# Joining two query tiles in one batch of scores, in the three attentions with 64-wide heads of a two-block transformer

## The reference

```python
# window: 8 query heads of width 64, 2 key heads; a key counts when |q - k| <= WINDOW (128); a sink joins the sum
s = jnp.einsum('bnqhgd,bnkhd->bnhgqk', qb, kb).astype(jnp.float32) * (ATT_HEAD_DIM ** -0.5)
s = jnp.where(valid[None, :, None, None], s, -jnp.inf)
m = jnp.maximum(jnp.max(s, axis=-1, keepdims=True), sk)
p = jnp.exp(s - m)
p = p / (jnp.sum(p, axis=-1, keepdims=True) + jnp.exp(sk - m))
# memory: 4 heads of width 256, 256 keys
# mla: 8 heads; two products make one score; key chunks up to the query's own
logits = (jnp.einsum('bqhd,bkhd->bhqk', qn, k_nope) + jnp.einsum('bqhr,bkr->bhqk', qp, k_pe))
# dsa: 8 heads of width 64; the 128 best keys of an index score, with a bias for each distance
logits = jnp.einsum('bqhd,bqkhd->bhqk', qb, k_sel).astype(jnp.float32) * scale
```

## Time and profile before

| | |
|---|---|
| Median of 3 runs | 1470.87 us (1466.79 to 1470.9) |
| The profiled execution | 1468.45 us, span 1466.6 us |
| PE busy | 1448.0 us (99%) |
| DVE / ACT / POOL busy | 935.8 / 447.4 / 833.2 us |
| window attention | about 276 to 360 us of the span |
| memory attention | about 496 to 592 us |
| mla attention | about 1123 to 1230 us |
| dsa attention | about 1254 to 1346 us |

### The profile page before, as it was taken

The page is one execution under the profiler, slowest core; times in us unless marked ns, Lnnn a source line. Parts: engine busy times, 40 slices in busy tenths (PEclk is TensorE's granted clock), DMA queues, the critical chain, the costliest instruction groups (busy, mean ns, idle before and its releaser), DMA issues.

```text
span 1466.6 us, 20029 instructions
## 1 busy us (share of the span) xinstructions
PE 1448.0 (99%) x7028; PEld 1149.8 (78%) x7028; DVE 935.8 (64%) x1685; ACT 447.4 (31%) x875; POOL 833.2 (57%) x675
## 2 busy tenths in 40 slices
PE   8999999999999999999999999999999999999998
PEld 7887877766888898788888888887767777667887
DVE  5768887777248334577777763325777786685245
ACT  4556432376122111220010101112333344464112
POOL 4634332534666786467777677776655254444662
PEclk9999999999999999999999999999999999999999
DMA  5211101211333433233333333334224532323332
GB/s 197 88 58 44 58 29 58 72 58 58 115 101 90 122 113 107 63 96 95 93 100 101 97 90 102 113 101 137 87 87 138 93 100 61 112 73 115 101 99 74
DMA packets 37017, 135.60 MB, mean 92 GB/s; under 512 B 4296, under 2 KB 4552, under 8 KB 36296
## 3 DMA queue, kind: packets, MB, share of 16 engines
q1 hardware_dynamic: 33264, 121.13, 27.4%
q10 hardware_dynamic: 3672, 13.35, 3.5%
HBM read 127.64 MB, written 6.82 MB: 92 GB/s over the span
## 4 chain that ended last, share of the span: by engine, by line
PE 89%; DVE 6%; issue 2%; ACT 1%; PEld 1%; DMA 0%; PEldq 0%; DVEq 0%
PE pair L624 25%; PE pair L626 24%; PE pair L625 24%; PE pair L909 4%; PE pair L937 3%; PE pair L921 2%; PE pair L798 1%; PE pair L785 1%; PE pair L833 1%; DVE dx L2112 1%; DVE selm L2388 0%; DVE dx L2109 0%; PE pair L744 0%; PE pair L743 0%; PE pair L820 0%
## 5 line engine op out<-in xcount | busy, mean ns | idle before, releaser
L579 POOL TENSOR_TENSOR wL<-ring,wH 128x1024 fp32r<-128x1024 f32 x223 | 547.8, 2457 | 18.6
L624 PE MATMUL pair<-nH,wH 128*128 128x512 f32 x1064 | 426.3, 401 | 2.1 <-DVE nL L1767 0.8
L626 PE MATMUL pair<-nH,wL 128*128 128x512 f32 x1064 | 414.9, 390 | 0.0
L625 PE MATMUL pair<-nL,wH 128*128 128x512 f32 x1064 | 414.8, 390 | 0.0
L576 POOL TENSOR_TENSOR tick<-tick 128x1 f32<-128x1 f32 x223 | 57.4, 258 | 591.2 <-PE pair L626 545.1
L624 PEld LDWEIGHTS pair<-nH,wH 128*128 128x128 f32 x1064 | 199.8, 188 | 62.7 <-issue 18.9
L577 POOL TENSOR_SCALAR wH<-ring 128x1024 fp32r<-128x1024 f32 x223 | 236.8, 1062 | 0.0
L626 PEld LDWEIGHTS pair<-nH,wL 128*128 128x128 f32 x1064 | 199.7, 188 | 42.4
L625 PEld LDWEIGHTS pair<-nL,wH 128*128 128x128 f32 x1064 | 199.9, 188 | 41.0 <-issue 1.9
L1610 ACT ACTIVATE sgb<-cv 128x512 f32<-128x512 f32 x22 | 13.9, 633 | 209.5 <-DVE cv L2297 209.5
L624 PE MATMUL pair<-aH,wH 128*128 128x512 f32 x176 | 68.5, 389 | 0.0
(11 more groups left out here) (409 smaller groups left out, 2652.4 us busy)
## 6 DMA issues: line engine op xcount, KB each, us to landing
ring<-stream SPq DMA_DIRECT2D x223, 512.0 KB, 3.5
gvec<-gv ACTq DMA_DIRECT2D x1, 2560.0 KB
hT<-xT SPq DMA_DIRECT2D x4, 512.0 KB, 6.0
x_d<-hT ACTq DMA_DIRECT2D x1, 2048.0 KB, 7.3
toep<-gvec ACTq DMA_DIRECT2D x8, 256.0 KB, 3.4
hT<-x_d ACTq DMA_DIRECT2D x1, 2048.0 KB, 8.2
out<-yo SPq DMA_DIRECT2D x4, 512.0 KB, 3.6
cD<-const_d ACTq DMA_DIRECT2D x1, 1345.0 KB, 6.3
```

The source lines that it names most:

```text
L579: pool.tensor_tensor(low, ring[:, r, :], high.bitcast(F32), ALU.subtract).then_inc(split_done, 1)
L624: mm(out, a[0], b[0], start=first, stop=False)
L625: mm(out, a[0], b[1], start=False, stop=False)
L626: return mm(out, a[1], b[0], start=False, stop=last)
```

## The change

The batches of an attention are now written in a table (`order`). In the window attention tiles 0 and 3 (2 and 2 blocks of keys) form one batch, then tile 1, then tile 2. In mla and dsa tiles 0 and 2 (1 and 3 blocks) form one batch, then tile 1, then tile 3. Both tiles of a joint batch lie in the same bank, one behind the other (`at`), one bank for each head of the pair (`side`), and the same holds for the rows in SBUF (`row`) and for the transposed probabilities. A head pair takes three steps instead of four, an attention 12 steps instead of 16. The joint step takes the shares of work beside of two old steps (`shares`). The memory attention keeps its order. Waits count units as before, but an engine that reads a bank waits for all units of the batch on that side (`side_done`), and one that writes it for all units of the batch before (`side_free`, `row_free`). The statistics get eight columns. The split buffers, the ring and the lags between steps stay.

```diff
+KINDS["window"]["order"] = [[0, 3], [1], [2]]
+KINDS["memory"]["order"] = [[i] for i in range(ST)]
+for _n in ("mla", "dsa"):
+    KINDS[_n]["order"] = [[0, 2], [1], [3]]
+def last_before(kind, x, same):
+
+    n = [y + 1 for y in range(x) if kind["batch"][y] != kind["batch"][x] and same[y] == same[x]]
+    return max(n, default=0)
...
+            kind["shares"].append([ST * (j // g) + share + n for n in range(len(tiles))])
...
+                    kind["side"].append(w if g == 2 else b % 2)
+                    kind["row"].append((2 * b + w) % 4 if g == 2 else b % 4)
+                    kind["at"].append(P * at)
...
+    kind["side_done"] = [max(y + 1 for y in kind["batches"][kind["batch"][x]] if kind["side"][y] == kind["side"][x]) for x in n]
+    kind["side_free"] = [last_before(kind, x, kind["side"]) for x in n]
...
-        stat = place("stat", [P, 4, 8])
+        stat = place("stat", [P, 8, 8])
...
-                    xs = range(group * s, group * s + group)
-                    if xs[-1] >= 2:
-                        pe.wait_ge(a_max, u0 + xs[-1] - 1)
...
+                    xs = kind["batches"][s]
+                    free = kind["side_free"][xs[-1]]
+                    if free:
+                        pe.wait_ge(a_max, u0 + free)
+                    for n_x in range(0, len(xs), group):
+                        tiles = []
+                        for x in xs[n_x:n_x + group]:
...
-                        beside(s)
+                        for n_b in kind["shares"][s]:
+                            beside(n_b)
...
-                    dve.wait_ge(a_sc, u + 1)
-                    if x >= 4:
-                        dve.wait_ge(a_turn, u - 3)
...
+                    dve.wait_ge(a_sc, u0 + kind["side_done"][x])
+                    if kind["row_free"][x]:
+                        dve.wait_ge(a_turn, u0 + kind["row_free"][x])
```

More of the change, by code:

```diff
@@ L197, with lay_out @@
     KINDS[_n]["serves"] = [(t, slice(P * t, S)) for t in range(ST)]
+KINDS["window"]["order"] = [[0, 3], [1], [2]]
[5 more added lines that the diff above has]
+    return max(n, default=0)
+def lay_out(kind, first):
+    g, heads, keys = kind["group"], kind["heads"], kind["keys"]
+    for name in ("units", "place", "batch", "side", "row", "at", "batches", "shares", "ends_head"):
+        kind[name] = []
+    for j in range(0, len(heads), g):
+        share = 0
+        for tiles in kind["order"]:
+            b = len(kind["batches"])
+            kind["batches"].append([])
+            kind["shares"].append([ST * (j // g) + share + n for n in range(len(tiles))])
+            share += len(tiles)
+            at = 0
+            for i in tiles:
+                for w in range(g):
+                    kind["batches"][b].append(len(kind["units"]))
+                    kind["units"].append((heads[j + w], i))
+                    kind["place"].append(j + w)
+                    kind["batch"].append(b)
+                    kind["side"].append(w if g == 2 else b % 2)
+                    kind["row"].append((2 * b + w) % 4 if g == 2 else b % 4)
+                    kind["at"].append(P * at)
+                at += keys(i)[1] - keys(i)[0]
+            kind["ends_head"].append(share == ST)
+    n = range(len(kind["units"]))
+    kind["side_done"] = [max(y + 1 for y in kind["batches"][kind["batch"][x]] if kind["side"][y] == kind["side"][x]) for x in n]
+    kind["side_free"] = [last_before(kind, x, kind["side"]) for x in n]
+    kind["row_free"] = [last_before(kind, x, kind["row"]) for x in n]
+    kind["first"], kind["first_head"] = first, first // ST
+    kind["lags"] = (3, 5, 7) if g == 1 else (1, 2, 3)
+    return first + len(kind["units"])
@@ L198 @@
 _u = 0
 for _k in KINDS.values():
[L200 to L205, removed]
+    _u = lay_out(_k, _u)
 DSA_ITEMS = [("q_b", c) for c in range(4)] + [("k_b", c) for c in range(4)] + [("v_b", j) for j in range(8)] + [
@@ L897, in scores @@
                 def scores(s):
-                    xs = range(group * s, group * s + group)
-                    if xs[-1] >= 2:
-                        pe.wait_ge(a_max, u0 + xs[-1] - 1)
[L902 to L911, removed]
+                    xs = kind["batches"][s]
[5 more added lines that the diff above has]
+                        for x in xs[n_x:n_x + group]:
+                            a, b = kind["keys"](units[x][1])
+                            at = kind["at"][x]
+                            tiles.append((bank(2 + kind["side"][x])[:, at:at + P * (b - a)], terms(*units[x], slice(P * a, P * b))))
+                        count = len(tiles[0][1])
+                        for t in range(count):
+                            for out, pairs in tiles:
+                                last = mm(out, *pairs[t], start=t == 0, stop=t == count - 1)
+                                if t == count - 1:
+                                    last.then_inc(a_sc, 1)
                 def turn_probs(x):
@@ L1476, in turned_probs @@
                     A(turned[:, j % 2, a:b, P * i:P * i + P],
-                      bank(4 + u % 2)[:, :P * (b - a)].rearrange("p (t q) -> p t q", q=P), ACT.Copy).then_inc(a_pt, 1)
-                steps = n // group
+                      bank(4 + kind["side"][x])[:, kind["at"][x]:kind["at"][x] + P * (b - a)].rearrange("p (t q) -> p t q", q=P),
+                      ACT.Copy).then_inc(a_pt, 1)
+                steps = len(kind["batches"])
                 for s in range(steps + out_lag + 2):
                     if s < steps:
-                        for x in range(group * s, group * s + group):
+                        for x in kind["batches"][s]:
                             exponents(x)
-                        beside(s)
+                        for n_b in kind["shares"][s]:
+                            beside(n_b)
                     elif s < steps + 2:
```

52 lines of the change are left out of this document (26 added, 26 removed).

## The result

The changed kernel takes 1470.86 us (median of 20 runs, 1468.85 to 1474.02) against 1468.41 us for the kernel before in the same session (20 runs, 1466.56 to 1471.20). The ratio is 1.0016, 95% interval 1.0009 to 1.0024: 2.4 us slower. The forecast was 1.2 us faster.

The account below looks back on a forecast made before the run. PE was taken to bound the kernel, busy 1448.0 of 1466.6 us. The terms -4.9+1.8+1.0+0.9 = -1.2 us took the median from 1470.87 to 1469.7 us, range 1464.8 to 1474.8.

Parts of the forecast that it names:

- The surcharge (-4.9): PE, three attentions: each head pair loses one burst of 64-row matmuls, 12 x 0.41 = -4.9 us, if switching tile is free.
- The third rival: PE's sequence isn't shortened: switching query tile costs as much as going in and out; 1474.6 us, chance 0.11.
- First pair of the window: Window's first head pair: DVE's normalisation meets POOL's split, PE waits 2.2 instead of 0.4 us, +1.8; between -0.1 and +1.8.
- First pair of DSA: DSA's first head pair: DVE sets the pace and starts later, so PE's wait before tile 3's scores grows, +1.0 us.
- The value copy in MLA: MLA's fourth head pair: the second share's transpose waits for the bank ACT's copy leaves after four exponents, +0.9 us.
- banks whose products ended a step before, so nothing waits: MLA's other pairs wait for no product bank, and ACT's later sigmoids stay covered; put at nothing.
- POOL's slots come at the same mean rate: Weight slots on POOL: said beside the 0.05 chance left for an unseen collision of transfers.
- PE waits nowhere in MLA before: MLA: said in costing DVE's doubled rounds of top keys in a joint step at nothing.
- Their number is drawn anew: DVE's stalls: where POOL's slots fall redraws their number; each is half the whole forecast, which fails if they move.
- a sign of being wrong: Profile after: waits on `stat` or `dx` in later head pairs would show the prediction wrong.
- The first rival: All of the surcharge is saved and the waits shrink too: -4.9 to -7.5 us, 1463.4 to 1466, chance 0.22.
- The second rival: Window and DSA: PE waits behind joint bursts' four maxima and normalisations, eight blocks of 1.3 us; +6.4, 1477.3 us, chance 0.14.

Follow-up runs that it names:

- e4: Changed kernel, with the first share's products on PE between the two tiles' scores, so the bursts are apart; 1488.37 us, 1.0143 of before.
- e5: Changed kernel, with a head pair's two shares in its last step and one beside the joint scores; 1471.60 us, 1.0031 of before.
- e8: Changed kernel, with the first share between the two tiles' maxima and exponents on DVE and ACT; 1468.21 us, 1.0000 of before.
- e9: Changed kernel, with joint steps and shares laid out pair by pair, MLA's pair 3 in four steps; 1463.96 us, 0.9964 of before.
- e10: Changed kernel, with GpSimd's 128x1024 subtraction written as four of 128x256; 1464.66 us, 0.9978 of before.

## Why the prediction was wrong, by its steps

**The surcharge (-4.9): right.** The joint burst saves 0.41 us in each pair without a new wait (window pairs 2 and 3, 20.56 and 20.62 us instead of 20.97 and 21.03), e4 takes it away and gets 21.01 back. The switch of query tile within a burst costs nothing visible: the joint burst of two tiles and eight records takes 1.06 us from its start to the next product's (293.84 to 294.90), a burst of one tile in e4 0.63 (299.25 to 299.88). The 0.43 between them is what the second tile's two passes of 256 columns take. The rule cited from the Trainium skill, "TensorEngine Tiling (Array Packing)", section Tiling Modes, is of changes of tiling mode, and both query tiles are scored in the same mode; these traces agree with it. The third rival falls.

**First pair of the window (+1.8 with its own burst not counted): too large.** The waits are 0.8 and 0.4 us instead of 0.4: +0.8; by the starts of the first scores (19.17 us from pair 1 to pair 2, before 18.40) it is +1.2 with the saved burst taken out. The stop came, but on the first normalisation (L2175 at 283.06, 2.40 us, behind L619 at 282.90), earlier than the prediction had it. The size was off, within the range given.

**First pair of DSA (+1.0): right in kind, too large.** It waits 1.3 us on `mtD` and 0.6 on `stat`, where before waited 1.8 in two pieces, so +0.1 in the view; by the starts of the first scores (19.24 us from pair 1 to pair 2, before 19.35) it is +0.3 with the saved burst taken out. The first wait stands at another place: at k=4's bank, which the first branch must leave, behind four maxima of which the first met the split (2.38 instead of 0.29 us).

**The value copy in MLA (+0.9): 0.5 in the view, 0.6 by the starts.** It is the L712 that was named.

**"... banks whose products ended a step before, so nothing waits. For the same reason ACT's later sigmoids (table load and 0.6 us) stay covered": this is the step that failed.** It put at nothing what turned out to be 1.5 us on MLA's first z_b gate, in the fourth pair, where the prediction looked only at the value copy. (In DSA's second pair a sigmoid costs 0.2 us too, L664 behind `sgD` at 1284.48.) The claim counted steps, not what PE does in them. The changed kernel, around the end of the first z_b product (PE without L665 and L666, then ACT, then DVE):

```profile
1213.20 0.39 PE L664 MATMUL pair<-nH,wH 128*128 128x512 f32 x1
...
1213.89 1.04 PE L964 MATMUL pair<-ident,dx 128*128 128x128 f32 x8
1214.85 0.70 PE L952 MATMUL pair<-kn,qn 64*128 64x256 f32 x4
1215.39 0.60 PE L952 MATMUL pair<-kpz,qp 64*128 64x256 f32 x4
1217.49 0.50 PE L664 MATMUL pair<-nH,wH 128*128 128x512 f32 x1 [1.50 <-DVE zb L1856]
...
1214.15 0.60 ACT L1339 ACTIVATE vB<-pair 128x512 f32<-128x512 f32 x1 [3.62 <-PE pair L666]
1214.77 1.28 ACT L1396 ACT_TABLE_LOAD   x1
1216.06 0.60 ACT L1396 ACTIVATE sgb<-pair 128x512 f32<-128x512 f32 x1
...
1216.75 0.69 DVE L1856 TENSOR_TENSOR zb<-pair,sgb 128x512 f32<-128x512 f32 x1 [1.51 <-issue]
```

From 1214.15 to 1217.44, 3.3 us in a row, ACT copies the value product, loads a table and makes the sigmoid, and DVE multiplies; only then is the bank free. DVE had ended its top keys at 1215.24 and waited for the sigmoid ("issue" hides this), so the doubled top keys are not to blame. The same chain took as long before (ACT's copy from 1216.39, DVE's product to 1219.67, again 3.3 us). What covered it then is PE's weighing of the pair ahead. The same place in the kernel before:

```profile
1215.44 0.39 PE L624 MATMUL pair<-nH,wH 128*128 128x512 f32 x1
1216.22 2.37 PE L937 MATMUL pair<-dPT,vA 128*64 128x512 f32 x16
1218.53 0.44 PE L921 MATMUL pair<-ident,dx 128*128 128x128 f32 x2
1218.89 0.92 PE L909 MATMUL pair<-kn,qn 64*128 64x384 f32 x4
1219.64 0.81 PE L909 MATMUL pair<-kpz,qp 64*128 64x384 f32 x4
1220.38 0.50 PE L624 MATMUL pair<-nH,wH 128*128 128x512 f32 x1
```

The weighing comes two steps after the last tile. Two steps were two shares (12 and 13); now the first of them holds both, the second holds share 14, and share 14 opens the bank before the weighing is reached. e5 moves the double share, so that the product ends in the step of the weighing again, and the wait is gone; e8 changes only the order in DVE and ACT, and it stays. No run moved the weighing alone, so that it is the weighing which is missing is read from the two sequences and from e5, not tested by itself.

**"POOL's slots come at the same mean rate" and "PE waits nowhere in MLA before": true, and no protection.** POOL and PE in the third pair, the changed kernel:

```profile
1175.64 0.19 POOL L616 TENSOR_TENSOR tick<-tick 128x1 f32<-128x1 f32 x1 [15.89 <-DMA ring<-stream]
1175.79 1.06 POOL L617 TENSOR_SCALAR wH<-ring 128x1024 fp32r<-128x1024 f32 x1
1176.93 2.38 POOL L619 TENSOR_TENSOR wL<-ring,wH 128x1024 fp32r<-128x1024 f32 x1
...
1179.45 0.47 PE L664 MATMUL pair<-nH,wH 128*128 128x512 f32 x1 [0.94 <-POOL wL L619]
```

A 512 KB load lands in 3.6 us over the kernel, but in 19.2 us here, while the 2560 KB store to `gvec` runs (in the kernel before in 19.4). The loads, in the whole trace and from 1150 to 1180 us:

```profile
ring<-stream SPq DMA_DIRECT2D x223, 512.0 KB, 3.6
...
ring<-stream SPq DMA_DIRECT2D x3, 512.0 KB, 19.2
```

POOL waited 15.89 us for its load, so DMA sets when the slot is there; two shares in a step ask for the second slot a burst and a transposition sooner.

**MLA's +2.3, added up.** Gate, slot and value copy make 2.9 us in the waits view; less 1.6 saved, that is only +1.3. The view is short, because it counts a wait from the end of the matmul before: that end is shown 0.39 us after its start, while without a wait the next would have started after 0.23. By the starts, against the same distance where nothing waits, the slot costs 1.2 us (1178.13 to 1179.45, 1.32 instead of 0.23, and 0.31 instead of 0.23 to the next), the copy 0.6 (1209.83 to 1210.67, 0.84 instead of 0.23), the gate 1.6 (1215.39 to 1217.49, 2.10 instead of 0.53), and the last tile's transposes, which no view lists as a wait, 0.5 (1.94 us from the product at 1233.83 to the one behind them, before 1.47). That makes 3.8, less 1.6 saved: +2.2.

**"Their number is drawn anew": right, and undersized.** The one meeting in DSA's third pair cost 1.8 us, more than the whole forecast, and made waits on `stat` in a later pair, which the prediction had named as a sign of being wrong. The first rival's gain exists (e9), but it takes other shares, not another fall of the splits. The second rival's mechanism, scores that wait behind four maxima, is seen in e5's DSA (7.0 us); where two shares cover them it is 0.2 us once, in DSA's third pair.

**The sum again, with what was measured by the starts:** -4.9 for the surcharge, +1.2 and +0.3 for the two first pairs, +0.6 for the value copy; then what was put at nothing: gate 1.6, slot 1.2, last transposes 0.5, the meeting in DSA 1.8. Together, with some of 0.2 to 0.4 us in both directions left out, +2.3 us, against 2.4 by the medians and 2.7 by the stages.

## What to carry to other kernels

Where stages lag each other by a count of steps, merging steps moves every lagged piece of work: list what stood between a product's end and the next use of its bank, by time and not by step, before and after. Merge step by step where the cover allows it, pair by pair, and add up stages from traces of variants rather than asking one rule of all. And look first at the stops between engines: here writing GpSimd's subtraction as four was worth 4.6 us to the kernel before, as much as the best layout of the steps (4.4).

## What the runs showed of the hardware

A VectorE instruction with two SBUF inputs that starts behind a GpSimd subtraction stands until that ends: 2.86 us for 0.69 when 0.05 us behind, 0.76 when 0.30 us ahead, 1.23 when GpSimd's instruction has a quarter of the columns. The same instruction with its scores in PSUM (`dx<-pair,cD`, all of MLA's) never stops: the longest of 448 in all 14 traces takes 0.69 us. Two SBUF tiles are not the only case, though: most of the stops in the attentions are normalisations (`dx<-dx,stat` and `wx<-wx,stat`, one tile and a column), 2.40 us for 0.35 at 283.06. The Trainium skill, "SBUF — State Buffer", section Who interferes with whom, says that VectorE and GpSimd share a pair of ports under an exclusive lock, that the first to issue holds it for a whole instruction, and that a VectorE instruction with two SBUF inputs contends with a GpSimd instruction that reads SBUF. By that rule cutting the instruction bounds the stop, and e10's trace agrees: 1.23 instead of 2.86 us. The price is a longer split: 128x1024 takes 2.46 us on average, four of 128x256 take 0.82 each, 3.3 in all.
